# First RMS norm of a two-layer encoder step: high parts first, squares after them, and the sum of squares inside the second projection job

## The reference, cut to what matters

```python
def rms_norm(x, g):
    xf = x.astype(jnp.float32)
    y = xf * lax.rsqrt(jnp.mean(xf * xf, axis=-1, keepdims=True) + EPS)
    return (y * g.astype(jnp.float32)).astype(x.dtype)

def proj_a(xn, w):
    B, L, _ = xn.shape
    q, k, v = jnp.split(xn @ w, [N_HEADS * HEAD_DIM, (N_HEADS + N_KV_A) * HEAD_DIM], axis=-1)
    return (q.reshape(B, L, N_HEADS, HEAD_DIM), k.reshape(B, L, N_KV_A, HEAD_DIM),
            v.reshape(B, L, N_KV_A, HEAD_DIM))
```

## Time and profile before

| | |
|---|---|
| median of 3 runs | 2971.2 us (2969.07 to 2971.53) |
| the profiled execution, its own time | 2970.41 us |
| its span in the profile | 2968.6 us |
| mean granted TensorE clock | 0.985 of full speed |
| PE busy | 2883.8 us, 97% |
| DVE, ACT, POOL busy | 1532.7, 679.5, 916.9 us (52, 23, 31%) |

### The profile page before, as it was taken

One profiled execution on the slowest core, in us unless ns is written; L12 is line 12 of the kernel. 1 busy time (PEld: TensorE's weight loads), 2 busy tenths in 40 slices (PEclk: granted clock), 3 DMA queues, 4 the chain that ended last, 5 costly groups with the idle time before them and its releaser, 6 DMA issues. The chain is left out here.

```text
span 2968.6 us, 47619 instructions
## 1 busy us (share of the span) xinstructions
PE 2883.8 (97%) x18423; PEld 2706.7 (91%) x18423; DVE 1532.7 (52%) x2815; ACT 679.5 (23%) x1327; POOL 916.9 (31%) x860
## 2 busy tenths in 40 slices
PE   8999999999999999999887999999999999999998
PEld 6987799999999999998487877789999999999997
DVE  5146624544444444455688777532644444444445
ACT  4035521000000000013467655532100000000002
POOL 4233333222222222224033754323222222222221
PEclk8999999999999999999999999999999999999998
DMA  4430011111111111114012000021111111111111
GB/s 123 66 96 10 22 29 36 36 36 42 42 42 42 42 42 42 36 43 130 1 35 72 11 10 9 20 80 37 37 42 42 42 37 41 42 42 38 39 36 74
DMA packets 178204, 129.78 MB, mean 44 GB/s; under 512 B 25313, under 2 KB 168353, under 8 KB 177846
## 3 DMA queue, kind: packets, MB, share of 16 engines
q1 hardware_dynamic: 178066, 127.90, 15.2%
HBM read 111.13 MB, written 15.16 MB: 43 GB/s over the span
## 5 line engine op out<-in xcount | busy, mean ns | idle before, releaser
L1215 POOL CAST w_hi<-w_raw 128x1024 fp32r<-128x1024 f32 x120 | 145.1, 1209 | 1111.8 <-PE ps_gemm L1450 606.9
L666 DVE TENSOR_TENSOR h<-h,ps_gemm 128x1170 f32<-128x1170 f32 x192 | 263.7, 1373 | 398.1 <-PE ps_gemm L1466 210.6
L1450 PE MATMUL ps_gemm<-xh,w_hi 128*128 128x390 f32 x1920 | 448.5, 341 | 0.0
L1450 PE MATMUL ps_gemm<-xh,w_lo 128*128 128x390 f32 x1920 | 448.1, 342 | 0.0
L1450 PE MATMUL ps_gemm<-xl,w_hi 128*128 128x390 f32 x1920 | 446.1, 340 | 0.0
L1450 PEld LDWEIGHTS ps_gemm<-xh,w_hi 128*128 128x128 f32 x1920 | 352.2, 189 | 0.1
L1450 PEld LDWEIGHTS ps_gemm<-xl,w_hi 128*128 128x128 f32 x1920 | 349.4, 189 | 0.0
L1450 PEld LDWEIGHTS ps_gemm<-xh,w_lo 128*128 128x128 f32 x1920 | 349.1, 189 | 0.0
L1218 POOL TENSOR_TENSOR w_lo<-w_raw,w_hi 128x1024 fp32r<-128x1024 f32 x120 | 289.5, 2413 | 17.4
L674 ACT ACTIVATE ac<-ac 128x1184 f32<-128x1184 f32 x44 | 52.5, 1194 | 863.2 <-DVE ac L731 863.2
L1414 PE MATMUL ps_gemm<-xl,w_hi 128*128 128x390 f32 x1056 | 246.5, 342 | 0.0
(11 more groups left out here) (411 smaller groups left out, 4716.1 us busy)
## 6 DMA issues: line engine op xcount, KB each, us to landing
w_raw<-in_w_gate SPq DMA_DIRECT2D x44, 512.0 KB, 3.8
w_raw<-in_w_up SPq DMA_DIRECT2D x44, 512.0 KB, 3.8
w_raw<-in_w_down SPq DMA_DIRECT2D x44, 512.0 KB, 3.5
w_raw<-in_w_in_b SPq DMA_DIRECT2D x13, 512.0 KB, 4.0
w_raw<-in_w_qkv_a SPq DMA_DIRECT2D x10, 512.0 KB, 4.0
residual_park<-h SPq DMA_DIRECT2D x1, 4680.0 KB, 13.6
h<-residual_park SPq DMA_DIRECT2D x8, 585.0 KB, 7.4
out<-yt SPq DMA_DIRECT2D x9, 512.0 KB
```

What stands on the lines that cost most here:

```text
L666: dve.tensor_tensor(c3(h[:, m, :]), c3(h[:, m, :]), pse(j), ALU.add).then_inc(evac[j % 2], 1)
L1215: pool.tensor_copy(whi[c % 3][:], raw[c % 2][:]).then_inc(w_hi_done, 1)
L1450: mm = pe.matmul(ps[j % 2][:, m_, 0:CH], w[:, k, :], x[:, k, m_ * CH:(m_ + 1) * CH], start=(k == 0 and w is wh and x is XH), stop=(k == KT ...
```

## The change

ACT makes all eight high parts of the first norm first and then the eight squares; DVE makes all eight low parts and then its three additions; PE does the square sum no longer between job 0 and job 1 but inside job 1, after the XH*whi and XL*whi products of tile 5. POOL's list stays as it is, and so do the three later norms and the final one.

```diff
+            def squares_between(k):
+
+                if k == 5:
+                    square_sum(0, G_X)
+
             pe.wait_ge(dve_setup, 1)
             for i, (kind, _, n) in enumerate(proj_a):
-                gemm(i, J_PA + i, XH, XL, n, gate=0 if i == 0 else None)
-                if i == 0:
-                    square_sum(0, G_X)
+                gemm(i, J_PA + i, XH, XL, n, gate=0 if i == 0 else None, between=squares_between if i == 1 else None)
                 if i == 1:
                     pe.wait_ge(ss_out, 3)
                     constants()
...
+
+                def high_part(k):
+                    copy(XH[:, k, :], h[:, k, :], gT[:, k, NORM_G[m]:NORM_G[m] + 1]).then_inc(xh_done, 1)
+
+                if m == 0:
+                    for k in range(KT):
+                        high_part(k)
                 for k in range(KT):
                     if m:
                         j = j_prev - KT + k
                         act.wait_ge(evac[j % 2], j // 2 + 1)
-                    if m < 4:
-                        copy(XH[:, k, :], h[:, k, :], gT[:, k, NORM_G[m]:NORM_G[m] + 1]).then_inc(xh_done, 1)
+                    if 0 < m < 4:
+                        high_part(k)
...
             for k in range(KT):
                 low_part(0, k)
+            for k in range(KT):
                 add_square(0, k)
             scale(0)
```

## The result

The changed kernel takes 2978.04 us (median of 8 runs, 2976.71 to 2982.87), the kernel before 2969.71 us (8 runs, 2968.23 to 2971.53): ratio 1.0028, 95% interval 1.0019 to 1.0037. It is 8.3 us slower; forecast were 8.9, and the median lies in the stated range of 2975.8 to 2982.3. The profiled execution took 2979.31 us, its span is 2977.5 (2968.6 before).

What follows compares the result with a forecast made beforehand. PE, busy 2883.8 of 2968.6 us, was taken to bound the kernel, its job 1 held by POOL's order of work. 1.0 + 2.0 + 2.5 + 3.0 + 0.4 = +8.9 us on 2970.41 gave 2979.3, range 2975.8 to 2982.3.

Steps and rivals of the forecast that it cites:

- Start of job 1: First norm: additions end later, POOL's split of chunk 1 follows, job 1 starts at 53.0 us, +1.0.
- the prediction's own sign: Profile after: the forecast is wrong if job 1 starts before 52, or job 2 follows the constants without a gap.
- The chain of additions: First norm, POOL and DVE: seven additions of squares in a strict row take 15.6 us, 22.2 before.
- the case that the prediction had chosen: POOL's first addition waits for DVE's running low part, so the additions end at 49.5 rather than 49.0 us.
- Clock at the start of job 1: PE idles before job 1, then runs some 4.5 us at half clock: +2.0 us (bounds 0 and 2.6).
- The square sum inside job 1: PE in job 1: the square sum loses its cover and delays the remaining 7 groups, +2.5 us.
- The new wait: Before job 2: PE waits for DVE to empty job 0's banks, +3.0 us, 2.2 without the sink subtraction meeting POOL's split.
- Clock at the start of job 2: After the constants and a wait, job 2 has 4.5 us at half clock instead of 3.6: +0.4 us.
- rival D: More than forecast: long half-clock stretches, later additions, a slow stretch in attention; +12.2 us, 2982.6, chance 9%.
- Rival A: Before job 2: the banks are empty in time, no wait; +5.5 us, 2975.9, chance 5%.
- rival B: Starts of job 1 and job 2: the clock stays at full speed; +4.9 us, 2975.3, chance 6%.
- Rival C: Faster: additions end much sooner, POOL splits chunk 1 earlier; 2966 with job 1 right behind job 0, chance 2%.

Runs made afterwards that it cites:

- e1: Changed kernel with POOL splitting weight chunk 1 before its additions of squares instead of after them: 2969.34 us, ratio 0.9994.
- e3: Changed kernel with the square sum back between job 0 and job 1, so only ACT's and DVE's new order: 2971.75 us, ratio 1.0002.
- e8: The changed kernel profiled and timed once more, nothing altered: 2979.38 us, ratio 1.0030.
- e10: Changed kernel plus 84 unused matmuls on PE between job 0 and job 1: 2978.74 us, ratio 1.0026.
- e4: Kernel before with only the square sum moved into job 1, at tile 5: 2978.57 us, ratio 1.0022.
- e5: Changed kernel with the square sum behind tile 0 of job 1 instead of tile 5: 2976.78 us, ratio 1.0020.
- e6: Changed kernel plus 74 unused matmuls on PE between job 0 and job 1: 2978.24 us, ratio 1.0023.
- e9: Changed kernel with POOL's split of chunk 1 first, square sum at tile 7, 16 unused matmuls behind the constants: 2967.32 us, ratio 0.9990.
- e7: Changed kernel with POOL's split of chunk 1 first and the square sum at tile 7 instead of 5: 2969.01 us, ratio 0.9995.

## Why the prediction was right

Point by point, in the profiled pair:

- *What bounds it.* Right: job 1 hangs on POOL's order (e1), and the earlier end of job 0 is worth nothing by itself (e3).
- *Start of job 1, +1.0.* The cause is right, the place 1.1 us off: measured 51.89 for a forecast of 53.0, 0.1 before the old start. By the prediction's own sign (wrong if job 1 starts before 52) that speaks against it. But the sign was set as a time from the start of the span, and 0.9 of the 1.1 us lie ahead of the norm, whose first high part began at 20.84 instead of 21.75. Counted from the first high part, job 1 started after 30.26 us before and after 31.05 in the changed kernel: +0.8. In e8, where the high parts began at 21.56, it started at 52.64, 0.6 later than before. The chain of additions took 15.4 us from the end of the low parts (22.14 + 10.88 = 33.02) to 48.45, for a forecast of 15.6: POOL's undisturbed addition is 2.65 here, not 2.73. The first one began while the last low part was running and took 3.13, which is the case that the prediction had chosen.
- *Clock at the start of job 1, +2.0.* Right in this pair: 11.32 us to the square sum, 2.0 more than 17 x 0.546; e10 measured 2.1. From one execution to the next the price varies: 1.5 in e8. And the prediction tied it to the early end of job 0 alone. e4, with the old order of high and low parts, lost 1.5 us there after 3.60 us of idling: the square sum's move would have brought most of this term by itself.
- *The square sum inside job 1, +2.5.* Measured 2.3: from 63.21 to 66.00 PE did the sum and one group of three (0.54).
- *The new wait, +3.0.* Measured 2.94, with kt as the releaser, and e5 takes it away. The meeting of the sink subtraction with POOL's split came (0.79 us for 16 columns), but cost 0.6 us where I had forecast 0.8.
- *Clock at the start of job 2, +0.4.* Measured: first q 15.22 us behind the start of job 2, 14.74 before: +0.5.
- *The sum.* -0.1 + 2.0 + 2.3 + 2.9 + 0.5 = 7.6, against 7.7 at the first q. The profiled spans differ by 8.9, the medians by 8.3. That the span hit the forecast to the tenth is chance: 1 us too much at the start of job 1, and 1.2 us more lost behind the first q, for which the sum had no term (3.0 us lost to the clock up to the second norm, 1.8 us won behind it; only rival D had a slow stretch in attention, at 1.6).

Rival A (no wait for the banks) and rival B (no fall of the clock) fell with the trace. Rival C was the interesting one: with another list for POOL (e1) the gap is closed, but the forecast of 2966 for it was too good (its own terms, 14 us off 2979.3, make 2965.3); e1 measured 2969.34, because the split and the low parts hold each other up.

## What to carry to other kernels

Before an engine's work is made earlier, look at who released its *next* job: if that is another engine's list, the gain ends in a wait there, and the fix belongs in that list. Work that stands in a wait is free only at that place; moved into a dense stretch it costs its full length, and everything that hangs on its result (here roots, reciprocals, the emptying of a bank) moves with it. An idle stretch of TensorE can cost a second time, at its end: here 1.5 to 2.7 us at the start of job 1, after 13.9 and 14.9 us of idling (e8 and the changed kernel), and after 3.6 (e4) and 3.0 us (e6) too.

## What I had not expected of the hardware

- A gap of 3.0 us, behind 13.3 us of dense full-clock matmuls, was enough for job 1 to begin at half clock (e6, granted clock 1.00 up to 49.8 and 0.50 from 52.8 to 57.9); with no gap to speak of it began at full clock (e10).
- Matmuls whose result nobody reads hold up or raise the clock for those that count: 16 of them, themselves at half clock, gave a full-clock start to job 2 (e9), where 5.6 us of waiting gave a half-clock one (e7).
- Where POOL's split and DVE's low parts meet, both lose: in e1 the cast takes 2.01 us instead of 1.04, the subtraction 3.41 instead of 2.35, and eight low parts, which meet POOL's first addition too, 16.3 us instead of 10.9. Even an instruction of 16 columns is held: the sink subtraction took 0.17 us alone (e5) and 0.79 to 1.79 beside a split (1.79 before, 1.62 in e7, 0.79 in the changed kernel).
